# Route stage of a decoder-layer kernel: the four one-hot arrays of a batch made on VectorE alone

## What is computed

```python
q = (xb @ wq).reshape(PEER_BLOCK, PEER_HEADS, 2, PEER_DHALF)
s = jnp.einsum('thcd,hcnd->thcn', q, subkeys).astype(jnp.float32)
sv, si = lax.top_k(s, PEER_TOPK)
cand = (sv[:, :, 0, :, None] + sv[:, :, 1, None, :]).reshape(...)
fv, fi = lax.top_k(cand, PEER_TOPK)
i1 = jnp.take_along_axis(si[:, :, 0], fi // PEER_TOPK, axis=-1)
i2 = jnp.take_along_axis(si[:, :, 1], fi % PEER_TOPK, axis=-1)
e = i1 * N_KEYS + i2
g = jax.nn.softmax(fv, axis=-1)
a = jax.nn.gelu(jnp.einsum('thkd,td->thk', u_tab[e], xb))
return jnp.einsum('thk,thkd->td', (g * a).astype(v_tab.dtype), v_tab[e])
```

## Time and profile before

| | before |
|---|---|
| median of 3 runs | 4511.48 us |
| profiled execution, its own time | 4522.91 us |
| span of the profiled execution | 4521.1 us |
| TensorE (PE) busy | 3564.3 us, 79% |
| VectorE (DVE) busy | 2525.8 us, 56% |
| ScalarE (ACT) busy | 759.6 us, 17% |
| GpSimd (POOL) busy | 693.6 us, 15% |
| mean granted clock of TensorE | 0.89 of 2.4 GHz |

### The profile page before, as it was taken

How to read it: one execution, slowest core, us unless ns; L and a number is a source line. 1 busy time by engine, 2 the same in 40 slices (tenths; PEclk the granted TensorE clock), 3 DMA queues, 4 the chain that set the end, 5 groups by cost and what they waited for, 6 DMA issues and landing times.

```text
span 4521.1 us, 60266 instructions
## 1 busy us (share of the span) xinstructions
PE 3564.3 (79%) x21641; PEld 2009.5 (44%) x21641; DVE 2525.8 (56%) x5218; ACT 759.6 (17%) x1241; POOL 693.6 (15%) x650
## 2 busy tenths in 40 slices
PE   4999646887765656227888898988889888898998
PEld 2555643444665555223334343443434434344354
DVE  3111544442777888835656565565655655556555
ACT  2110222211001111111111111111111111111122
POOL 0000000000002333331221212212122121221101
PEclk8999768998876666559999999999999999999999
DMA  6211333333000222257776777767777777777622
GB/s 174 80 68 59 108 133 143 115 108 132 15 10 5 79 79 74 74 177 295 270 299 255 285 287 282 296 255 284 285 281 293 264 279 269 279 300 268 240 98 97
DMA packets 274890, 835.65 MB, mean 185 GB/s; under 512 B 38088, under 2 KB 143856, under 8 KB 213200
## 3 DMA queue, kind: packets, MB, share of 16 engines
q0 software_dynamic: 64512, 469.79, 27.2%
q1 hardware_dynamic: 210272, 364.48, 23.7%
HBM read 742.12 MB, written 93.39 MB: 185 GB/s over the span
## 4 chain that ended last, share of the span: by engine, by line
PE 28%; DMA 9%; DVE 6%; DVEq 5%; issue 4%; ACT 1%; SPq 1%; POOL 1%; PEld 0%; POOLq 0%; ACTq 0%; PEldq 0%
PE experts_ps L1532 12%; PE experts_ps L1519 8%; PE experts_ps L1505 5%; DMA experts_ut<-in_uT 4%; DMA experts_rows<-in_uv,experts_place 4%; PE experts_ps L1494 3%; DVEq L1660 3%; DVE experts_prod L1657 2%; DVEq L1685 1%; DVE experts_hl L1688 1%; DVE experts_hf L1684 1%; DVEq L1667 1%; DVE experts_hh L1686 1%; ACT experts_act_a L1571 1%; DMA experts_shift<-in_ln_b 1%
## 5 line engine op out<-in xcount | busy, mean ns | idle before, releaser
L1598 POOL DMA_INDIRECT experts_rows<-in_uv,experts_place x448 | 454.1, 1014 | 1810.1 <-PE experts_ps L1505 1684.7
L1519 PE MATMUL experts_ps<-experts_xh,experts_uh 128*128 128x320 f16 x2048 | 622.2, 304 | 77.7 <-DMA experts_eye<-in_c_eye 55.7
L1657 DVE CUSTOM_DVE_ANT_0 experts_prod<-experts_rows,experts_ps 128x1024 f32<-128x1024 f32 x448 | 545.2, 1217 | 148.4 <-DMA experts_rows<-in_uv,experts_place 98.6
L1519 PE MATMUL experts_ps<-experts_xl,experts_uh 128*128 128x320 f16 x2048 | 619.9, 303 | 0.0
L1519 PE MATMUL experts_ps<-experts_xh,experts_ul 128*128 128x320 f16 x2048 | 619.3, 302 | 0.0
L1532 PE MATMUL experts_ps<-experts_vh,experts_hh 128*128 128x512 f16 x1280 | 489.5, 382 | 3.0 <-DVEq L1689 2.8
L1532 PE MATMUL experts_ps<-experts_vl,experts_hh 128*128 128x512 f16 x1280 | 486.8, 380 | 0.0
L1532 PE MATMUL experts_ps<-experts_vh,experts_hl 128*128 128x512 f16 x1280 | 486.2, 380 | 0.0
L1697 DVE SCALAR_TENSOR_TENSOR experts_y<-experts_ps,experts_y 128x512 f32<-128x512 f32 x320 | 221.0, 691 | 451.8 <-PE experts_ps L1532 440.3
L1494 PE MATMUL experts_ps<-experts_xr,experts_pick 32*128 32x512 f16 x896 | 271.9, 383 | 242.3 <-DVE experts_dot L1657 240.6
L1519 PEld LDWEIGHTS experts_ps<-experts_xh,experts_uh 128*128 128x128 f16 x2048 | 202.1, 99 | 274.4 <-issue 182.4
(11 more groups left out here) (252 smaller groups left out, 5145.5 us busy)
## 6 DMA issues: line engine op xcount, KB each, us to landing
experts_ut<-in_uT SPq DMA_DIRECT2D x128, 512.0 KB
experts_vt<-in_uv SPq DMA_DIRECT2D x128, 512.0 KB, 4.9
scratch_g<-route_gbuf SPq DMA_DIRECT2D x5, 8192.0 KB, 30.4
experts_g<-scratch_g SPq DMA_DIRECT2D x128, 320.0 KB, 3.2
scratch_z<-project_z SPq DMA_DIRECT2D x10, 1984.0 KB, 7.1
project_piece<-in_w_in SPq DMA_DIRECT2D x15, 1024.0 KB, 5.7
merge_w_piece<-in_w_merge SPq DMA_DIRECT2D x13, 1024.0 KB, 7.6
mix_za<-scratch_z SPq DMA_DIRECT2D x10, 960.0 KB, 5.6
```

The costliest lines, as they stand in the source:

```text
L1519: mm = pe.matmul(ps[:, p % 2, 0:W], w[:, m % 2, t, :], x[:, t, c * W:(c + 1) * W], start=t == 0 and j == 0, stop=t == KT - 1 and j == 2)
L1598: pool.indirect_dma_start(rows[:, t % RING], None, a.uv.rearrange("r e d -> (r e) d"), bass.IndirectOffsetOnAxis(ap=place[:, t:t + 1], axi ...
L1657: dve.tensor_tensor_reduce(prod[:].rearrange("p (c n) -> p c n", c=2), rows[:, q % RING, 0:D].rearrange("p (c n) -> p c n", c=2), ps[:, 4: ...
```

## The change

VectorE makes hot_l itself, behind hot_h and from the same two operands, and GpSimd has no work left in the stage. The drain between hot_r and hot_c goes behind hot_c. The semaphores `rows_ready` and `lows_ready` go, with TensorE's wait for the latter. At a block's head, VectorE's wait that `gl` is free becomes one for TensorE's last group of the block before (`g_full`).

```diff
-        one, scrap = s.sb("one", [P, 1]), s.sb("scrap", [P, 1])
...
-        rows_ready, lows_ready = s.sem("rows_ready"), s.sem("lows_ready")
...
                         pe.wait_ge(hots_ready, d * batches + b + 1)
-                        pe.wait_ge(lows_ready, d * batches + b + 3)
...
-            @block.gpsimd
-            def _(pool):
-                pool.memset(one[:], 1.0)
-                pool.drain()
-                pool.sem_inc(lows_ready, 2)
...
-                    def batch(b, half):
-                        pool.wait_ge(rows_ready, d * batches + b + 1)
-                        pool.tensor_tensor(scrap[:], one[:], one[:], ALU.mult)
-                        pool.tensor_tensor(hot_l[:, half], hot_r[:, half], spread(gl[:, bass.ds(b * BT, BT)]), ALU.mult)
-                        pool.drain().then_inc(lows_ready, 1)
-                    over_batches(pool, batch)
...
-                    dve.wait_ge(lows_ready, d * batches + 2)
+                    dve.wait_ge(g_full, d * batches * 2 + 4)
...
                         dve.tensor_tensor(hot_r[:, half], numbers, spread(col[:, 0, now]), ALU.is_equal)
-                        dve.drain().then_inc(rows_ready, 1)
                         dve.tensor_tensor(hot_c[:, half], numbers, spread(col[:, 1, now]), ALU.is_equal)
+                        dve.drain()
                         dve.tensor_tensor(hot_h[:, half], hot_r[:, half], spread(gh[:, now]), ALU.mult)
+                        dve.tensor_tensor(hot_l[:, half], hot_r[:, half], spread(gl[:, now]), ALU.mult)
                         dve.drain().then_inc(hots_ready, 1)
```

More of the change, by code:

```diff
@@ L1197, in _ @@
                 over_steps(act, body)
-            @block.gpsimd
-            def _(pool):
-                pool.memset(one[:], 1.0)
-                pool.drain()
-                pool.sem_inc(lows_ready, 2)
-                def body(k, d, last):
-                    if d is None:
-                        return
-                    def batch(b, half):
-                        pool.wait_ge(rows_ready, d * batches + b + 1)
-                        pool.tensor_tensor(scrap[:], one[:], one[:], ALU.mult)
-                        pool.tensor_tensor(hot_l[:, half], hot_r[:, half], spread(gl[:, bass.ds(b * BT, BT)]), ALU.mult)
-                        pool.drain().then_inc(lows_ready, 1)
-                    over_batches(pool, batch)
-                over_steps(pool, body)
             @block.vector
```

## The result

The changed kernel took 4443.49 us (median of 4 runs, 4430.75 to 4451.89) against 4513.08 for the one before on the same chip (4 runs, 4511.46 to 4517.01): ratio 0.9842, 95% interval 0.9815 to 0.9869. The profiled execution took 4430.75 us. Over all runs of this study the means are 4441.2 us (14 runs) and 4512.8 us (40 runs; with the profiled execution of 4522.91 us, which is not among them, 4513.1), 71.6 us apart. The forecast was 4434, with 77.8 us gained.

The account below looks back on a forecast made before the run. VectorE was taken to bound the route stage. A batch falling from 4.36 to 3.28 us saves 1.08 in 72 batches, 77.8 us off the median 4511.48, giving 4434 us, range 4419 to 4457.

Parts of the forecast that it names:

- The wait in hot_h: VectorE's multiply making hot_h in the route stage: its 2.38 us is mostly waiting while GpSimd's instruction reads.
- x = 0.69: Time in us of one 1024-element VectorE multiply (hot_h or hot_l) alone, with GpSimd idle; bounded by 0.69 and 2.38.
- The rivals with x at 1.23 and 2.38: Route-stage multiplies at one element per cycle, 4511 us, chance 0.04; or dear in themselves, 4689 us, chance 0.03.
- strict reading of the step rule: For the multiplies: a repeated operand has a step of 0 somewhere and would fall to the lower rate.
- The pairs overlap: On VectorE, the two compares and the two multiplies each start 0.61 us apart, start to start.
- The batch: One route-stage batch on VectorE takes 3.28 us, 1.08 less than 4.36.
- 72 of 80 batches: Batches 0 and 1 of four blocks gain nothing, waiting for TensorE's scores; 72 batches gain 1.08 us each, 77.8 us.
- Nothing else late: TensorE (2.03 us a batch), ScalarE (1.2 us), stores and the block-head wait don't become late at 3.28 us a batch.
- The experts stage gives it back: Rival: the stage behind the route stage eats the gain, anywhere from 4434 to 4511 us; chance 0.04.

## Why the prediction was right, point by point

*The wait in hot_h.* The prediction read 2.38 us as 0.69 of work behind GpSimd's read, from the compare of the same shape and from the 0.55 between the two ends. hot_h alone takes 0.692, and the runs with GpSimd's multiply, copy and memset show that its reads, and neither its signal nor its being busy, are what hold VectorE.

*x = 0.69.* Measured 0.692 and 0.684. The rivals with x at 1.23 and 2.38 are out, and with them the prediction's strict reading of the step rule: the repeated operand doesn't bring these multiplies to the lower rate.

*The pairs overlap.* Starts 0.61 apart within both pairs, as taken.

*The batch.* 3.20 and not 3.28: 0.15 behind the drain where 0.21 was taken, and 0.01 to 0.02 less elsewhere. Per batch 1.16 us are gained.

*72 of 80 batches.* Right: the wait at the third batch grew to 4.29 us in four blocks (about 4.1 foreseen), the last block has none. 72 x 1.16 = 83.5 us, and the route stretch shrank by 83.6.

*Nothing else late.* Right inside the stage: VectorE waits for no one in the middle of a block, and the stretch from the last store to the experts stage is unchanged.

*The experts stage gives it back*, a rival with a chance of 0.04, came true in part: some 12 of the 83.5 us. My argument against it was that nothing ahead of the stage changes but the time of its start. VectorE's code ahead of it changes too, and about half of the loss stands where VectorE's pauses go with that code; the rest of it stays open. The sum 83.5 - 12 = 71.5 lies within 7 us of the forecast 77.8 partly by luck, because two misses cancel: the batches gained 6 more than I had, the experts stage took 12.

## What to carry to other kernels

An instruction that takes several times what its sibling of the same shape takes, the same in every case, and that ends a fixed time behind another engine's instruction, is waiting and not working: price a change by the sibling. Moving part of a bounding engine's work to GpSimd can cost more than the part itself, if both then read SBUF at once; taking 80 instructions back onto the bounding engine made it faster. And judge a stage's gain by its own stretch of the trace as well as by the total: a later stage that the edit doesn't touch gave a seventh of it back here. A run that adds instructions to give time back changes the program too, so it is no clean test of the time alone.

## What the runs showed that I had not expected

The hold goes both ways, and by who starts first: GpSimd's multiply of one element went from 0.19 to 0.57 us when it started inside hot_c, and in the run with the moved drain hot_h, 0.06 us ahead of GpSimd, was not held at all. Whoever is held on VectorE ends 0.54 to 0.55 us behind GpSimd, in all four kernels where it happens. So hot_l's 2.40 us on GpSimd before the change may have held a wait for hot_c too; a GpSimd multiply that starts behind hot_c takes 1.89. That one reads constants without a repeated operand, so the operand could also be the difference; no run parts the two.
